# The transposes of a U block in one group, behind one copy, in the fused loop of a PEER layer

## The reference, cut to what matters

```python
def block(ht):
    T = ht.shape[0]
    q = (ht @ w_q).reshape(T, PEER_HEADS, 2, PEER_HALF)
    s1 = jnp.einsum('thd,hkd->thk', q[:, :, 0], keys1).astype(jnp.float32)
    s2 = jnp.einsum('thd,hkd->thk', q[:, :, 1], keys2).astype(jnp.float32)
    v1, i1 = lax.top_k(s1, PEER_TOPK)
    v2, i2 = lax.top_k(s2, PEER_TOPK)
...
    top, pos = lax.top_k(cand, PEER_TOPK)
    eidx = jnp.take_along_axis(cidx, pos, axis=-1)
    gate = jax.nn.softmax(top, axis=-1)
    ug = u[eidx]
    act = jax.nn.gelu(jnp.einsum('thkd,td->thk', ug, ht).astype(jnp.float32), approximate=False) * gate
    vg = v[eidx]
    return jnp.einsum('thk,thkd->td', act.astype(ht.dtype), vg)
```

## Time and profile before

| | us |
|---|---|
| median of 3 runs (1564.23 to 1567.38) | 1564.39 |
| span of the profiled execution | 1563.7 |
| PE busy in it | 1512.8 (97%) |
| DVE busy | 1401.7 (90%) |
| ACT busy | 596.5 (38%) |
| POOL busy | 493.3 (32%) |

### The profile page before, as it was taken

One profiled execution on the slowest core, in us unless ns is written; L12 is line 12 of the kernel. 1 busy time (PEld: TensorE's weight loads), 2 busy tenths in 40 slices (PEclk: granted clock), 3 DMA queues, 4 the chain that ended last, 5 costly groups with the idle time before them and its releaser, 6 DMA issues.

```text
span 1563.7 us, 23267 instructions
## 1 busy us (share of the span) xinstructions
PE 1512.8 (97%) x8404; PEld 1281.7 (82%) x8404; DVE 1401.7 (90%) x2988; ACT 596.5 (38%) x968; POOL 493.3 (32%) x422
## 2 busy tenths in 40 slices
PE   7999999899999999999999999999999999999996
PEld 5455654788899999999898999999999899787885
DVE  5887987799999999995999999999999999989997
ACT  3104431521555445543333333333333333334343
POOL 1000000232010411010555565555555555343330
PEclk9999999999999999999999999999999999999998
DMA  9864232230465788789999999999999999999993
GB/s 325 287 217 148 101 138 59 81 98 38 136 212 154 261 262 256 251 278 313 408 396 396 402 401 410 407 397 398 399 407 404 385 402 375 362 406 377 398 391 121
DMA packets 180570, 455.71 MB, mean 291 GB/s; under 512 B 15020, under 2 KB 81700, under 8 KB 178280
## 3 DMA queue, kind: packets, MB, share of 16 engines
q1 hardware_dynamic: 113600, 231.84, 41.2%
q0 software_dynamic: 57632, 209.78, 34.9%
q10 hardware_dynamic: 9224, 12.62, 2.4%
HBM read 421.63 MB, written 32.25 MB: 290 GB/s over the span
## 4 chain that ended last, share of the span: by engine, by line
PE 55%; DVE 13%; DMA 4%; issue 2%; ACT 1%; DVEq 0%; SPq 0%; POOL 0%; ACTq 0%; POOLq 0%
PE peer_psum L1656 13%; PE peer_psum L1660 7%; PE peer_psum L1716 6%; PE peer_psum L1723 6%; PE peer_psum L1731 6%; PE peer_psum L1668 4%; PE peer_psum L1703 3%; PE peer_psum L1720 3%; PE peer_psum L1726 3%; DVE s_all L1807 2%; DMA s_all<-in_peer_v 2%; PE peer_psum L1641 1%; DVE s_all L1902 1%; DVE s_in L1906 1%; DVE s_all L1904 1%
## 5 line engine op out<-in xcount | busy, mean ns | idle before, releaser
L1656 PE MATMUL peer_psum<-hH,hi_slots 128*128 128x320 f32 x1024 | 307.3, 314 | 5.1 <-ACT hi_slots L1599 2.1
L1656 PE MATMUL peer_psum<-hL,hi_slots 128*128 128x320 f32 x1024 | 302.0, 309 | 0.0
L1527 POOL DMA_INDIRECT hT<-in_peer_u,eidx x128 | 146.6, 1145 | 292.0 <-DVE dots L1798 251.5
L1563 ACT ACTIVATE hi_slots<-s_all 128x1024 fp32r<-128x1024 f32 x128 | 135.9, 1062 | 189.2 <-PE peer_psum L1731 172.0
L1527 POOL DMA_INDIRECT hT<-in_peer_v,eidx x128 | 149.6, 1169 | 177.6 <-DVE s_all L1807 164.7
L1656 PEld LDWEIGHTS peer_psum<-hH,hi_slots 128*128 128x128 f32 x1024 | 192.6, 188 | 9.7 <-issue 5.2
L1656 PEld LDWEIGHTS peer_psum<-hL,hi_slots 128*128 128x128 f32 x1024 | 192.6, 188 | 3.1 <-issue 0.2
L1660 PE MATMUL peer_psum<-hH,lo_slots 128*128 128x320 f32 x1024 | 171.2, 309 | 2.1 <-DVE lo_slots L1845 2.1
L1935 DVE TENSOR_TENSOR lo_slots<-s_all,hi_slots 128x1024 fp32r<-128x1024 f32 x128 | 156.3, 1221 | 17.5 <-ACT hi_slots L1563 15.9
L1807 DVE SCALAR_TENSOR_TENSOR s_all<-hT,coef,s_all 128x1024 f32<-128x1024 f32 x126 | 161.3, 1280 | 3.3 <-DMA hT<-in_peer_v,eidx 2.9
L1660 PEld LDWEIGHTS peer_psum<-hH,lo_slots 128*128 128x128 f32 x1024 | 156.6, 188 | 5.1 <-DVE lo_slots L1845 2.6
(11 more groups left out here) (318 smaller groups left out, 2856.6 us busy)
## 6 DMA issues: line engine op xcount, KB each, us to landing
ring<-in_peer_u SPq DMA_DIRECT2D x128, 512.0 KB
s_all<-in_peer_v SPq DMA_DIRECT2D x128, 512.0 KB
gate_table<-lot SPq DMA_DIRECT2D x16, 1280.0 KB, 7.1
lot<-gate_table SPq DMA_DIRECT2D x16, 1280.0 KB
gelu_table<-s_all ACTq DMA_DIRECT2D x56, 160.0 KB
s_in<-gelu_table SPq DMA_DIRECT2D x56, 160.0 KB
x_sb<-in_w_mod POOLq DMA_DIRECT2D x8, 1024.0 KB, 8.2
lot<-in_peer_wq SPq DMA_DIRECT2D x8, 1024.0 KB, 5.6
```

The source lines that it names most:

```text
L1527: pool.indirect_dma_start(rows_of(j), None, A[table][0], bass.IndirectOffsetOnAxis(eidx[:, k:k + 1], 0)).then_inc(rows_in[j % RG], 16)
L1563: func(H[:, slot_of(w), :], vb[:, w % RING, :], ACT.Copy).then_inc(v_hi, 1)
L1656: mm(ps[:, bank, 0:TD], H[:, b, c * P:(c + 1) * P], h[:, c, T0:T], start=(c == 0 and h is hH), stop=False)
```

## The change

In the fused loop the two groups of four transposes become one of eight, after `value(w, 0)`, and both banks are written there, so the whole group waits for the gelu of the block before. One ACT copy of 1024 columns takes the place of two of 512. DVE makes the low part in two halves behind this copy, with one row between them; the gated product comes first in its turn, and `value_low` of a V block moves from the end of a turn to the next turn, behind the product. `value` is called in three parts; the order of its matmuls stays. In the lead, the transposes of the blocks in `LOW_BY_DVE` carry start and stop flags each (the plain form).

```diff
+        turned = ps[:, 6:8, :].rearrange("p a n -> p (a n)")
@@ ACT, fused loop
-                if n < NBLK:
-                    act.wait_ge(half_turned, n - LEAD + 1)
-                    act.wait_ge(u_done, n)
-                    func(H[:, 0, 0:512], ps[:, 6 + n % 2, :], ACT.Copy).then_inc(ua_high, 1)
...
                 if n < NBLK:
                     act.wait_ge(u_turned, n + 1)
-                    func(H[:, 0, 512:D], ps[:, 7 - n % 2, :], ACT.Copy).then_inc(ub_high, 1)
+                    act.wait_ge(u_done, n)
+                    func(H[:, 0, :], turned, ACT.Copy).then_inc(both_high, 1)
@@ PE, lead_turn
                 for c in range(DC):
-                    last = mm(uT_of(b)[:, c * P:(c + 1) * P], ub[:, n % RING, c * P:(c + 1) * P], ident[:], is_transpose=True,
-                              start=(c % 4 == 0), stop=(c % 4 == 3), skip_group_check=True)
+                    into, of = uT_of(b)[:, c * P:(c + 1) * P], ub[:, n % RING, c * P:(c + 1) * P]
+                    if n in LOW_BY_DVE:
+                        last = tr(into, of, ident[:])
+                    else:
+                        last = mm(into, of, ident[:], is_transpose=True, start=(c % 4 == 0), stop=(c % 4 == 3), skip_group_check=True)
@@ PE, fused loop
-            def turn(n, half):
-                for c in range(4):
-                    last = tr(ps[:, 6 + (n + half) % 2, c * P:(c + 1) * P], ub[:, n % RING, (4 * half + c) * P:(4 * half + c + 1) * P], ident[:])
-                last.then_inc((half_turned, u_turned)[half], 1)
+            def turn(n):
+                for c in range(DC):
+                    last = tr(turned[:, c * P:(c + 1) * P], ub[:, n % RING, c * P:(c + 1) * P], ident[:])
+                last.then_inc(u_turned, 1)
...
-                if n < NBLK:
-                    pe.wait_ge(u_in[n % RING], 16 * (n // RING + 1))
-                    turn(n, 0)
                 if w >= 0:
                     value(w, 0)
                 if n < NBLK:
+                    pe.wait_ge(u_in[n % RING], 16 * (n // RING + 1))
                     if n > LEAD:
                         pe.wait_ge(s_ready, n)
-                    turn(n, 1)
+                    turn(n)
                 if w >= 0:
                     value(w, 1)
+                if w >= 0:
+                    value(w, 2)
                 if n < NBLK:
-                    pe.wait_ge(ua_high, n - LEAD + 1)
-                    pe.wait_ge(ub_high, n - LEAD + 1)
-                    pe.wait_ge(ua_low, n - LEAD + 1)
+                    pe.wait_ge(both_high, n - LEAD + 1)
+                    pe.wait_ge(half_low, 2 * (n - LEAD) + 1)
                     scores_high(6 + n % 2, 0)
-                    pe.wait_ge(ub_low, n - LEAD + 1)
+                    pe.wait_ge(half_low, 2 * (n - LEAD) + 2)
                     scores_low(6 + n % 2, 0)
@@ DVE, fused loop
-                if n < NBLK:
-                    dve.wait_ge(ua_high, n - LEAD + 1)
-                    v.tensor_tensor(L[:, 0, 0:512], ps[:, 6 + n % 2, :], H[:, 0, 0:512].bitcast(F32), ALU.subtract).then_inc(ua_low, 1)
...
-                if n < NBLK:
-                    if left > 3:
-                        take_row()
-                        left -= 1
-                    dve.wait_ge(ub_high, n - LEAD + 1)
-                    v.tensor_tensor(L[:, 0, 512:D], ps[:, 7 - n % 2, :], H[:, 0, 512:D].bitcast(F32), ALU.subtract).then_inc(ub_low, 1)
-                    if left > 1:
-                        take_row()
-                        left -= 1
-                elif w < NBLK:
+                if 1 <= w and n <= NBLK:
+                    value_low(w - 1)
+                if n >= NBLK and w < NBLK:
                     value_low(w)
...
                 if n < NBLK:
-                    if left > 1:
-                        take_row()
-                        left -= 1
-                    if w >= 0:
-                        value_low(w)
+                    dve.wait_ge(both_high, n - LEAD + 1)
+                    for i in range(2):
+                        k = (n + i) % 2
+                        part = slice(k * 512, k * 512 + 512)
+                        v.tensor_tensor(L[:, 0, part], ps[:, 6 + k, :], H[:, 0, part].bitcast(F32), ALU.subtract).then_inc(half_low, 1)
+                        if i == 0 and left > 1:
+                            take_row()
+                            left -= 1
                 for _ in range(left):
                     take_row()
```

More of the change, by code:

```diff
@@ L1418, in peer_block @@
              "coef_ready"))
-        (u_turned, half_turned, u_high, u_less, u_low, u_low_dve, ua_high, ua_low, ub_high, ub_low, u_done, s_ready, v_hi, v_lo, v_done, c_done,
+        (u_turned, u_high, u_less, u_low, u_low_dve, both_high, half_low, u_done, s_ready, v_hi, v_lo, v_done, c_done,
          a_ready, a_hi, a_lo, yc_done, folded, y_sq, out_ready) = (sem(n) for n in (
-             "u_turned", "half_turned", "u_high", "u_less", "u_low", "u_low_dve", "ua_high", "ua_low", "ub_high", "ub_low", "u_done", "s_ready",
+             "u_turned", "u_high", "u_less", "u_low", "u_low_dve", "both_high", "half_low", "u_done", "s_ready",
              "v_hi", "v_lo", "v_done", "c_done", "a_ready", "a_hi", "a_lo", "yc_done", "folded", "y_sq", "out_ready"))
@@ L1716, in value @@
                             mm(y_bank(g, h), aH[:, NB + g * P:NB + (g + 1) * P], H[:, s, h * 512:(h + 1) * 512], start=first, stop=False)
-                else:
+                elif part == 1:
                     pe.wait_ge(a_lo, w + 1)
```

## The result

The median of the runs is 1586.76 us (1584.52 to 1590.46, 4 runs) against 1564.31 us before; the ratio is 1.0147, 95% interval 1.0124 to 1.0169. The change makes the kernel slower by 1.5%. The forecast was 1567.1 us with a range up to 1573.5: the direction it leaned to was right, the size was not. The profiled execution has a span of 1588.3 us, 24.6 more than the one before. By ACT's gelus that divides into 0.6 before the fused loop, 0.7 in its first two turns, 19.9 in the other 70 (from its third gelu to its last), and 3.4 after it.

The account below looks back on a forecast made before the run. PE was taken as busy all the time in the fused loop, with 8.13 us turns. Grouping -0.85, stalls +2.6 and loop ends +1.0 gave +2.75 us on a profiled 1563.7, 1567.1 as median; range 1560.5 to 1573.5.

Parts of the forecast that it names:

- The lead: Transposes before the fused loop change only their flags, 25 blocks of 56: price 0, at most 0.25 us either way.
- The usual turn: Quiet fused turn: wide copy starts at T+2.00, first low half at T+3.06, nothing waits, length 8.12 to 8.13 us.
- The first two turns: Start of the fused loop, where PE already waits for the copies: +0.4 us in turn one, +0.3 in turn two.
- the point from which PE notices: DVE's product may start at T+1.45 at most before PE waits for value's low part; usual start T+0.80 or T+0.91.
- With the five lags above the stalls become: Late gathered rows in the fused loop: five lags from the old trace give PE stalls of 4.6 for 2.0, +2.6 us.
- Queues: SP's V load moves next to U and gate loads, POOL's gathers are freed in a bunch: price 0, upper bound +7.
- The clock falls: Rival, chance 0.01: PE's granted clock goes to half for one turn in ten, +57 us.
- the DVE work per turn: Fused turn on DVE: work unchanged, 7.8 us with dot-product rows and 7.92 with weighted rows, only the order changes.
- rival D: Chance 0.08: DVE's product settles beyond T+1.45, or s_ready stops PE, so every fused turn grows, about 1574 us.
- a saving of 0.85: Transposes in one group on PE: one switch fewer saves 0.012 us a turn, 0.85 us over 70 turns.
- Rival C: Chance 0.20: DMA binds, late places grow by about 1 us and new ones appear at gate loads, 1571 to 1574 us.
- its last turn: Turn 128, without transposes: part 2 is due at T+2.32, its low part ready at T+2.57, +0.3 us.

Follow-up runs that it names:

- the spread one: Changed kernel with DVE's rows put back between its other work and the V block's low part in its own turn, V loads earlier too: 1569.66 us, ratio 1.0027.

## Why the prediction was wrong

**What was right.** The lead, nothing (the plain form alone: 1.0001). The usual turn: copy at T+2.00, low half at T+3.06, length 8.12 to 8.13. The first two turns, +0.34 and +0.32 where 0.4 and 0.3 were named. And the point from which PE notices: I put it at a product started at T+1.45. In the long turns it starts at T+3.78, 3.84, 1.96, 3.23, 4.17, 3.17 and 3.98; less 1.45 that is 2.33, 2.39, 0.51, 1.78, 2.72, 1.72 and 2.53, and the turns were over by 2.33, 3.95, 0.51, 1.79, 4.28, 1.72 and 4.09. Four fit to 0.01 us, and the other three are 1.56 longer, behind the half clock. So the mechanism of the forecast, late rows that reach PE sooner, is what happened. The direction was right by it, and not by luck.

**What failed, first: the lags taken over from the old trace.** The step "With the five lags above the stalls become", with 4.6 as its outcome, used 1.81, 1.30, 1.25, 2.16 and 1.02. Under the changed kernel there are seven lags, five of them over 2.4 (counted from the forecast's own usual start, T+0.80 or T+0.91), and without the clock's share the stalls sum to 14.0. In "Queues" I had priced the traffic at 0 with an upper bound of +7, for a V load that moves next to the U and gate loads and for gathers freed in a bunch. Measured, the waits for rows nearly doubled, 8.9 to 16.9 us. Moving the V loads alone raised them by 4.8 on the old kernel and by 2.6 on the spread one; spreading the rows with the V loads back in time took off 5.0; cutting the gate loads took off 11.1. That the lump of the gate load is what makes rows late is shown, by its removal and by its splitting. The 5.0 divide into 2.4 for DVE's order at nearly equal V loads (16.9 to 14.5; U and V are swapped on SP) and 2.6 for the V loads at equal DVE order (14.5 to 11.9), one profile each, so this division leans that way and is not settled; nor is where the 3.0 from 8.9 to 11.9 come from. In time the division is clear: of the loop's 17.2 us between the same two ends, 15.5 go with DVE's order, with less room for a late row (0.54 or 0.65 us before PE stands, where there were 1.1), chained rows, and three falls of the clock behind its stalls.

**Second: the clock.** The rival "The clock falls" was given 0.01, and the only cause that the prediction named for a fall was a longer group of transposes. The clock did fall, but behind stalls: 3 x 1.56 = 4.7 us. A stall's price is thus not always its length. This step was missing from every rival.

**Third: the DVE work per turn "is the same".** It was not. I took a weighted row at its place in the old order, with other work behind it. Side by side, two of the three take 1.38 to 1.39 from start to start, since each waits for the end of the one before and reads its sum; that is 2 x 0.19 us, DVE needs 8.33 a turn and not 7.92, the product starts at T+1.64 and not at T+0.91, beyond the T+1.45 that I had set myself as the limit. That is rival D's standing wait, at 0.08, and in the 19 turns it cost 3.9 us. The old trace shows it, in a pair of weighted rows in its tail, 1.38 apart:

```profile
1347.85 1.28 DVE L1807 SCALAR_TENSOR_TENSOR s_all<-hT,coef,s_all 128x1024 f32<-128x1024 f32 x1
1349.23 1.28 DVE L1807 SCALAR_TENSOR_TENSOR s_all<-more_rows,coef,s_all 128x1024 f32<-128x1024 f32 x1
```

**The sum, put right.** 18.7 - 2.2 for late rows (4.7 of it clock) and 3.9 for chained rows is 20.4; less 0.5, which the quiet turns gave back, it is the 19.9 measured. The forecast had 2.6 for late rows, nothing for chained ones, and a saving of 0.85. Rival C came nearest in kind, and its own sign, waits for rows over some 9 us, came true. Its 1571 to 1574 lacked clock and chain, and was too small even without them: late rows alone, without the clock, cost 11.8 us more than before, where C had 2.6 and 4 to 7. Of the 3.4 us after the loop 1.3 are the fall of the clock shown above, where the forecast had 0.3 for its last turn. The rest stays open: the kernel before has 237.5 us behind its last gelu in one profile and 235.0 in that of the run with plain transposes in the lead, which has the same tail, against 240.9 in the changed kernel.

## What to carry to other kernels

When an order is changed, the lags of the old trace are no fixed input if the change also moves transfers or makes rows be used in a bunch (8.9 us of waits became 16.9). Work out for each engine how much lag its consumer takes before it stalls: here that number, T+1.45, was right to 0.01 us, and the lags put into it were not. A large transfer that comes once in several turns may be worth cutting in pieces where the DMA engines are busy all the time: here it gave 0.3% on the old kernel and four fifths of the loss on the changed one. An accumulating instruction that reads the sum of the one before was cheaper here with other work between the two, 1.20 against 1.38 us.

## What the runs showed that I had not expected

Behind the stalls of three of the seven long turns of the changed kernel, and one in its tail, the granted clock was half for 3.4 us, costing 1.56 us each in the loop; with the two stalls at the start of the loop it was at half for 3.4 us (five times) or for 6.8 us (four times) in nine of the eleven experiments' profiles, and not there in the other two, nor in those of the kernels before and after. Which of them it strikes I cannot tell from the trace: a stall of 2.08 us in the loop and one of 2.11 in the kernel before had no fall behind them, one of 2.08 in the tail had. A faster DVE loop (two accumulators) did not shorten the loop of the changed kernel by anything, 591.5 against 591.2 us, with waits for gathers at 20.2 against 16.9 us. Weighted rows: 1.19 to 1.20 us start to start with other work behind, 1.38 to 1.39 with a row that adds to the same sum.
